# Bias sums at expert pair 9 instead of 12, the last pair's running sums put into PSUM earlier, and the last combine and statistics taken half by half

## The chip, the cores and the metric

The kernel runs on one core of one Trainium2 chip. The metric is the time on the device in microseconds (us). The profile is that of one profiled execution of its own, whose time and span stand beside each other below. TensorE is written PE, its weight loads PEld, VectorE DVE, ScalarE ACT, GpSimd POOL, SyncE SP.

## The reference

One step of a decoder with one layer (`DEPTH` = 1), in float32, for 256 prompt rows and 32 sample rows (8 sequences of 4 tokens), 288 rows of 1024 columns in all:

```python
proj = x @ w_in                         # q, k, v of two head groups
o    = w_out applied to concat(RMSNorm_head(o_A) * gn_moba, RMSNorm_head(o_B) * gn_win)
hx   = LayerNorm(alpha * x + o)         # ln1
logits = hx @ w_router + b_router; the top 4 of 32 experts, softmax over the 4 -> comb (rows x 32)
for each expert e:                      # w_gate_up 1024 x 2048, w_down 1024 x 1024
    gu   = hx @ w_gate_up[e] + b_gate_up[e]
    gate = min(gu[:, 0::2], 7); up = clip(gu[:, 1::2], -7, 7)
    act  = gate * sigmoid(1.702 * gate) * (up + 1)
    acc += comb[:, e] * (act @ w_down[e] + b_down[e])
y    = LayerNorm(alpha * hx + acc)      # ln2
```

The outputs are y for prompt and sample rows and the new key and value rows and window buffers.

## The kernel before

**Stages.** Attention and the first LayerNorm come first. After them the 32 experts are done as 16 pairs (`PAIRS`), numbered 0 to 15; this is most of the time. Each expert takes up to 64 rows (`SLOTS`), so a pair fills 128 slots. If some expert has more than 64 rows, further passes follow (`further_passes`); the profiled execution has none.

**One pair on TensorE.** `gather` picks the pair's rows by a matmul with 0/1 matrices (lines 1051 and 1055). `turn_slots` transposes them, ACT copies them to `xg`. `begin_gate_up` puts the biases of the first projection into banks 0 to 3 (L1267). `gate_up` runs k = 0 to 7, and for each k 8 matmuls 128x64 by 128x512, each of which the trace shows as two instructions (L1171; 64 instructions are four k). DVE and ACT make SwiGLU of it (`swiglu`, `sigmoids`). `turn_act` transposes `up`, ACT copies it to `actT`. `down` runs v = 0 to 3 with two j each (L1224), into banks 4 and 5. ACT copies the result to `ybuf`. `combine` multiplies it by `spread` (the slots' gates, which spread slots over rows): ten matmuls (L1251, L1237), added by DVE to `acc` and `acc_s` (L2080). In a pair that isn't the last, `combine(i)` is issued inside `gate_up(i + 1)` after k = 3.

**The weights.** They come in units of 2 MB, 12 to a pair (u = 0 to 7 the first projection, 8 to 11 the second), into a ring of 9 places (`RING`), all issued by SP in one queue. A unit is issued when the one nine before it has been used (`unit_free`). In pairs 1 to 14 (`load_whole`) two units belong together, and PE waits for both of them ahead of k = 0, 2, 4, 6 and v = 0, 2. In pairs 0 and 15 each unit serves one k or v. Of pair 15, unit 11 comes as two halves, one for each of its j (`load_last_pair`, L523). When `gate_up` of pair 15 is done, the gains and biases of the last LayerNorm are loaded (`load_last`).

**Bias sums.** `finish_with_biases(MIDDLE, ...)` with `MIDDLE` = 12 puts into the `down` of pair 12 the transposition of `comb`, and comb x b_down (plus alpha x ln1_b) for all rows: four 33x128 by 33x512 matmuls and four small ones (`add_biases`, L1122, `add_sample_biases`, L1129). DVE adds them to `acc` (`add_biases`, L2088), and PE waits for that ahead of `gate_up(13)`.

**The last pair (15).** `gate_up` with `combine(14)` after k = 3 and `turn_weights` after k = 5. Then `last_down`: the first half of `up` is transposed (L732), and while ACT copies it PE moves the running sums of tile 0 and of the samples into PSUM by matmuls with the identity (`keep_sums`, L1331 and L1330). After v = 0 and v = 1 the sums of tile 1 follow. Then, when v = 3 is done, ACT copies one half of the result to `ybuf` and DVE the other. `mix_last` adds the combination to the sums in PSUM (L1373), first both halves of tile 0, then the samples, then tile 1. DVE takes the statistics (L2160, L2167), ACT the roots; ACT centres tile 0, DVE multiplies by the gain (L2186), POOL adds the bias, and DVE does samples and tile 1. SP stores.

**Order.** Every engine's program is written out by hand, in order, with semaphores between them. PE never runs past a wait.

Of the kernel before, what the change touches and what calls it, by code (L numbers as in the profile page):

```python
# [109 lines left out]
def build_layer(nc, x_prompt, x_sample, cache_k, cache_v, state_k, state_v, page_table, w_in, gn_moba,  # L110
# [9 lines left out]
    def place(name, shape, at=None, dt=F32):  # L120
# [90 lines left out]
        wout_in2 wout_in3 k_landed0 k_landed1 k_landed2 k_landed3 v_landed0 v_landed1 v_landed2 v_landed3 ln1_in  # L211
# [10 lines left out]
        unit5 unit6 unit7 unit8 unit_used first_in att_in blk_in gn_in bias_in bias_used picked gathered xtok_ready  # L222
# [3 lines left out]
        sums_whole copies_out  # L226
# [100 lines left out]

    def pair_of(p):
        return slice(2 * p, 2 * p + 2) if isinstance(p, int) else bass.ds(p * 2, 2)
# [36 lines left out]
    MIDDLE = 12  # L366
# [35 lines left out]
    def _(sp):  # L402
# [107 lines left out]
        def load_last_pair():  # L510
# [11 lines left out]
            for c in range(2):  # L522
                sp.dma_start(dst[:, :, c, :], src[:, :, 2 + c, :]).then_inc(half_in[8 + c], 16)  # L523
# [22 lines left out]
        sp.dma_start(ln_g[:, :], ln1_g[0:1, :].broadcast_to([128, D])).then_inc(S.ln1_in, 16)  # L546
# [183 lines left out]
    def _(pe):  # L730
# [41 lines left out]
        def mean_squares(n):  # L772
            pe.wait_ge(S.out_taken, n + 1)
            if n == 0:
                pe.wait_ge(S.blk_in, 32)
# [340 lines left out]
        def add_biases(j):  # L1116

            t, half = divmod(j, 2)
            if j == 0:
                pe.wait_ge(S.combT_ready, 2)  # L1120
                pe.wait_ge(S.bdn_in, 32)
# [112 lines left out]
        def mix_samples(out, start):  # L1234

            for q in range(4):
# [86 lines left out]
        finish(MIDDLE + 1, MIDDLE // PERIOD, 1, MIDDLE // PERIOD)  # L1323
        last = PAIRS - 1
        finish(last - 1, last // PERIOD - 1, 2, None)

        def keep_sums(t, half, stop=False):

            if t == 2:
                return nc.tensor.matmul(bank[7][:, 0:256], ident, acc_s[:, :], start=True, stop=stop)  # L1330
            return nc.tensor.matmul(bank[2 * t + half][:, :], ident, acc[:, t, 512 * half:512 * half + 512],  # L1331
                                    start=True, stop=stop)
# [894 lines left out]
```

## Time and profile before

| | us |
|---|---|
| median of 3 runs | 1140.02 |
| lowest, highest | 1139.33, 1140.36 |
| profiled execution | 1139.37 |
| its span | 1137.5 |

| engine | busy us | share |
|---|---|---|
| PE | 1099.5 | 97% |
| DVE | 293.1 | 26% |
| ACT | 203.6 | 18% |
| POOL | 30.0 | 3% |

The span is cut by the page into 40 slices of 28.4 us. From the eighth slice on, its line of DMA rates reads 407 to 433 GB/s, until the last one (160 GB/s). A busy share says how long an engine had an instruction in it, not that the end of the program waits for it. The chain of waits follows the last instruction back to what released it, step by step.

### The profile page before, as it was taken

How to read it: one execution, taken by the hardware profiler on the slowest of the kernel's cores; microseconds unless marked ns; L12 is line 12 of the kernel's file. 1: busy time of each engine (PE TensorE's matmuls, PEld its weight loads, DVE VectorE, ACT ScalarE, POOL GpSimd, SP SyncE). 2: the span in 40 equal slices, each digit the busy share in tenths (PEclk: the TensorE clock that was granted, in tenths of full speed). 3: DMA queues.
4: the chain of work that ended last, by engine and by line, in shares of the span. 5: the costliest groups of instructions: out<-in, count | busy, mean ns of one | idle time of the engine just before them, and what ended most of it. 6: DMA issues, size and time to landing. Idle time of an engine off the chain costs nothing.

```text
span 1137.5 us, 14116 instructions
## 1 busy us (share of the span) xinstructions
PE 1099.5 (97%) x5468; PEld 463.2 (41%) x5469; DVE 293.1 (26%) x734; ACT 203.6 (18%) x481; POOL 30.0 (3%) x65
## 2 busy tenths in 40 slices
PE   8999999999999999999999999999999999999996
PEld 6876764433333333333333333333333333333331
DVE  1553757530303030212121212120203031303033
ACT  2323412411111120202020202020201111111102
POOL 0110111000000000000000000000000000000001
PEclk9999999999999999999999999999999999999998
DMA  9967878999999999999999999999999999999994
GB/s 361 351 219 248 285 280 336 426 433 407 430 421 430 430 431 430 431 430 429 432 431 432 432 430 432 432 432 429 433 430 432 432 430 432 431 430 430 425 426 160
DMA packets 59172, 454.37 MB, mean 399 GB/s; under 512 B 6467, under 2 KB 19411, under 8 KB 31348
## 3 DMA queue, kind: packets, MB, share of 16 engines
q1 hardware_dynamic: 56642, 440.97, 92.7%
q0 software_dynamic: 1728, 10.75, 2.5%
q10 hardware_dynamic: 754, 1.98, 0.4%
q8 instruction: 34, 0.56, 0.2%
q14 instruction: 14, 0.11, 0.0%
HBM read 450.14 MB, written 11.93 MB: 406 GB/s over the span
## 4 chain that ended last, share of the span: by engine, by line
PE 83%; DMA 13%; ACT 2%; DVE 2%; issue 1%; SPq 0%; DVEq 0%
PE bank L1171 30%; PE bank L1224 19%; DMA ring<-in_w_gate_up 13%; PE bank L732 6%; PE bank L759 6%; PE bank L1055 5%; PE bank L1251 3%; PE bank L762 2%; PE bank L920 2%; PE bank L1051 1%; PE bank L1354 1%; PE bank L1267 1%; PE bank L877 1%; ACT ybuf L1417 1%; ACT actT L1417 1%; PE bank L851 1%
## 5 line engine op out<-in xcount | busy, mean ns | idle before, releaser
L1171 PE MATMUL bank<-ring,xg 128*64 128x512 f32 x2032 | 445.6, 594 | 10.8 <-DMA ring<-in_w_gate_up 10.8
L1171 PEld LDWEIGHTS bank<-ring,xg 128*64 128x64 f32 x2032 | 146.4, 137 | 299.3 <-issue 296.9
L1224 PE MATMUL bank<-ring,actT 128*64 128x512 f32 x960 | 216.2, 597 | 4.2 <-ACT actT L1417 4.2
L2080 DVE TENSOR_TENSOR acc<-acc,bank 128x512 f32<-128x512 f32 x60 | 41.3, 688 | 492.0 <-PE bank L1251 491.8
L1571 ACT ACTIVATE sig<-gate 128x256 f32<-128x256 f32 x64 | 26.5, 416 | 530.1 <-DVE gate L2062 530.1
L1224 PEld LDWEIGHTS bank<-ring,actT 128*64 128x64 f32 x960 | 67.3, 137 | 120.0 <-issue 115.3
L2062 DVE TENSOR_SCALAR gate<-bank 128x256 f32<-128x256 f32 x64 | 26.8, 419 | 186.8 <-PE bank L1171 186.8
L759 PE MATMUL bank<-xT,wblk 128*128 128x288 f32 x256 | 65.4, 409 | 0.3 <-DVE xT L1670 0.3
L1562 ACT ACTIVATE xg<-bank,small 128x128 f32<-128x128 f32 x128 | 48.0, 457 | 97.0 <-PE bank L732 96.9
L1055 PE MATMUL bank<-hx,pick 128*128 128x512 f32 x128 | 59.2, 605 | 0.0
L1417 ACT ACTIVATE ybuf<-bank 128x512 f32<-128x512 f32 x63 | 36.0, 596 | 126.7 <-PE bank L1224 87.4
L1251 PE MATMUL bank<-ybuf,spread 128*128 128x512 f32 x120 | 58.4, 619 | 0.0
L759 PEld LDWEIGHTS bank<-xT,wblk 128*128 128x128 f32 x256 | 47.5, 190 | 14.6 <-issue 2.7
L1055 PEld LDWEIGHTS bank<-hx,pick 128*128 128x128 f32 x128 | 23.0, 190 | 34.3 <-issue 34.3
L1251 PEld LDWEIGHTS bank<-ybuf,spread 128*128 128x128 f32 x120 | 19.2, 189 | 39.0 <-DVE acc L2080 19.7
L920 PE MATMUL bank<-wout,outT 128*128 128x512 f32 x64 | 29.8, 603 | 0.0
L762 PE MATMUL bank<-wblk,xT 128*128 128x256 f32 x128 | 29.0, 380 | 0.0
L2066 DVE SCALAR_TENSOR_TENSOR up<-up,gate 128x256 f32<-128x256 f32 x64 | 27.2, 425 | 3.3
L732 PEld LDWEIGHTS bank<-keep,ybuf 128*128 128x128 f32 x128 | 17.8, 207 | 25.3 <-issue 24.3
L723 POOL TENSOR_TENSOR acc<-acc,ln_b_sb 128x512 f32<-128x512 f32 x2 | 3.0, 1500 | 941.0 <-DVE acc L2186 941.0
L2063 DVE TENSOR_SCALAR up<-bank 128x256 f32<-128x256 f32 x64 | 26.5, 414 | 0.0
L2071 DVE TENSOR_TENSOR up<-up,sig 128x256 f32<-128x256 f32 x64 | 25.4, 419 | 0.0
(247 smaller groups left out, 672.3 us busy)
## 6 DMA issues: line engine op xcount, KB each, us to landing
ring<-in_w_gate_up SPq DMA_DIRECT2D x127, 2048.0 KB, 26.5
ring<-in_w_down SPq DMA_DIRECT2D x63, 2048.0 KB, 28.0
wblk<-in_w_in SPq DMA_DIRECT2D x11, 1024.0 KB, 8.7
kring<-in_cache_k_moba SPq DMA_DIRECT2D x16, 256.0 KB, 7.5
vring<-in_cache_v_moba SPq DMA_DIRECT2D x16, 256.0 KB, 7.2
out<-in_state_k_win POOLq DMA_DIRECT2D x8, 512.0 KB, 5.2
out<-in_state_v_win POOLq DMA_DIRECT2D x8, 512.0 KB, 6.1
kring<-in_state_k_win SPq DMA_DIRECT2D x16, 256.0 KB, 5.3
```

The costliest lines, as they stand in the source:

```text
L732: return nc.tensor.transpose(out, in_, ident[0:in_.shape[0], 0:in_.shape[0]])
L759: ins = nc.tensor.matmul(out[:, 0:T], w[:, k, 128 * c:128 * c + 128], xT[:, k, :], start=(k == 0), stop=(k == KC - 1))
L762: ins = nc.tensor.matmul(out[:, 0:256], xT[:, k, 128 * c:128 * c + 128], w[:, k, :], start=(k == 0), stop=(k == KC - 1))
L920: return nc.tensor.matmul(bank[2 * t + half][:, :], outT[:, k, t0:t0 + rows], wout[:, k, 512 * half:512 * half + 512], start=(k == 0), sto ...
L1055: return nc.tensor.matmul(bank[6 + a][:, :], pick[:, t, :], hx[:, t, 512 * a:512 * a + 512], start=False, stop=(t == 1))
L1171: ins = nc.tensor.matmul(bank[n][64 * e:64 * e + 64, :], xg[:, k, 64 * e:64 * e + 64], w[e][:, 512 * n:512 * n + 512], start=False, stop=( ...
L1224: ins = nc.tensor.matmul(bank[4 + half][64 * e:64 * e + 64, :], actT[:, j, 64 * e:64 * e + 64], w[e][:, at:at + 512], start=(j == 0), stop ...
L1251: ins = nc.tensor.matmul(bank[4 + half][:, :], spread[:, t0:t0 + rows], ybuf[:, 512 * half:512 * half + 512], start=True, stop=True)
L1417: return nc.scalar.activation(out, in_, ACT.Copy, **kw)
L1562: ins = nc.scalar.activation(xg[:, k, :], turned, ACT.Identity, bias=s_(c_cols + KC + k), scale=s_(c_cols + k))
L2066: V.scalar_tensor_tensor(up[:, c], up[:, c], 1.0, gate[:, half_of(n)], ALU.add, ALU.mult).then_inc(S.dve_moe, 1)
L2080: V.tensor_tensor(o, o, new, ALU.add).then_inc(S.added, 1)
```

## The change

`MIDDLE` goes from 12 to 9, and the pairs 10 to 13 are then written out behind the loop. In the last pair `combine(14)` comes after k = 1 instead of k = 3, and the sums of tile 0 and the samples are put into PSUM after k = 4 of `gate_up` (`keep_first`) instead of inside `last_down`. The banks of the last pair change for that: the result of `down` goes to banks 0 and 1 (`Y_BANK`), the sums of tile 0 to banks 4 and 5, those of tile 1 to 2 and 3, those of the samples to 7 (`SUM_BANK`); both halves of `up` are transposed through bank 6 (`turn_last`). The part of unit 11 for its second j (1 MB) comes by column halves, as two transfers of 512 KB with rows of 2 KB instead of 4 KB. PE signals when the lower half of `down` is done, ACT copies both halves one after the other (`take_halves`), and DVE copies none. `mix_last` goes half by half: tile 0, tile 1 and two of the samples' quarters of the lower half, then the same of the upper one. DVE takes the lower halves' statistics first. The wait for the last LayerNorm's gains moves down to where they are read. Two semaphores go: `ln1_in` is merged into `bdn_in`, `att_in` into `blk_in`, so what waited for the one transfer now waits for three.

```diff
-    MIDDLE = 12
+    MIDDLE = 9
@@ load_last_pair
-            for c in range(2):
-                sp.dma_start(dst[:, :, c, :], src[:, :, 2 + c, :]).then_inc(half_in[8 + c], 16)
+            sp.dma_start(dst[:, :, 0, :], src[:, :, 2, :]).then_inc(half_in[8], 16)
+            for half in range(2):
+                h = slice(512 * half, 512 * half + 512)
+                sp.dma_start(dst[:, :, 1, h], src[:, :, 3, h]).then_inc((S.lower_in, half_in[9])[half], 16)
@@ sync, scalar
-        sp.dma_start(ln_g[:, :], ln1_g[0:1, :].broadcast_to([128, D])).then_inc(S.ln1_in, 16)
+        sp.dma_start(ln_g[:, :], ln1_g[0:1, :].broadcast_to([128, D])).then_inc(S.bdn_in, 16)
-        act.dma_start(att[:, :], att_table[:, 0:A_END]).then_inc(S.att_in, 16)
+        act.dma_start(att[:, :], att_table[:, 0:A_END]).then_inc(S.blk_in, 16)
...
-                    act.wait_ge(S.att_in, 16)
+                    act.wait_ge(S.blk_in, 48)
...
-                dve.wait_ge(S.att_in, 16)
+                dve.wait_ge(S.blk_in, 48)
...
-            dve.wait_ge(S.ln1_in, 16)
+            dve.wait_ge(S.bdn_in, 48)
@@ tensor: the pairs after the biases
         finish_with_biases(MIDDLE, MIDDLE // PERIOD, 0, MIDDLE // PERIOD)
         finish(MIDDLE + 1, MIDDLE // PERIOD, 1, MIDDLE // PERIOD)
+        finish(MIDDLE + 2, MIDDLE // PERIOD, 2, MIDDLE // PERIOD + 1)
+        finish(MIDDLE + 3, MIDDLE // PERIOD + 1, 0, MIDDLE // PERIOD + 1)
+        finish(MIDDLE + 4, MIDDLE // PERIOD + 1, 1, MIDDLE // PERIOD + 1)
@@ tensor: the last pair
-        def last_down():
-
-            turn_act(last, 2 * last + 2, (0,))
+        def keep_first():
             pe.wait_ge(S.added, 5 * last + 5)
             keep_sums(0, 0)
             keep_sums(0, 1)
-            pe.wait_ge(S.actT_ready, last * 2 + 1)
             keep_sums(2, 0)
+
+        def turn_last(a):
+            pe.wait_ge(S.act_ready, last * 4 + 2 * a + 2)
+            pe.wait_ge(*((S.actT_ready, 2 * last + 1) if a else (S.spread_ready, last + 1)))
+            for j in range(4 * a, 4 * a + 4):
+                f = 512 * a
+                ins = turn(bank[6][:, 128 * (j % 4):128 * (j % 4) + 128], up[:, f + j % 4:f + 512:4])
+            ins.then_inc(S.act_turned, 1)
+
+        def last_down():
+
+            turn_last(0)
...
-                    if v == 3:
-                        pe.wait_ge(half_in[8 + c], 16)
+                    if j == 6:
+                        pe.wait_ge(half_in[8], 16)
                     for half in range(2):
+                        if j == 7:
+                            pe.wait_ge((S.lower_in, half_in[9])[half], 16)
                         for e in range(2):
                             at = 2048 * e + 1024 * c + 512 * half
-                            ins = nc.tensor.matmul(bank[4 + half][64 * e:64 * e + 64, :], actT[:, j, 64 * e:64 * e + 64],
+                            ins = nc.tensor.matmul(bank[Y_BANK[half]][64 * e:64 * e + 64, :], actT[:, j, 64 * e:64 * e + 64],
                                                    w[:, at:at + 512], start=(j == 0), stop=(j == KC - 1))
+                        if j == 7 and half == 0:
+                            ins.then_inc(S.lower_done, 1)
...
-            pe.wait_ge(S.y_ready, last * 2 + 2)
-            for j in (0, 1, 4, 2, 3):
...
+            for half in range(2):
+                pe.wait_ge(S.y_ready, last * 2 + half + 1)
+                for t in range(2):
+                    nc.tensor.matmul(bank[SUM_BANK[t][half]][:, :], spread[:, 128 * t:128 * t + 128],
+                                     ybuf[:, 512 * half:512 * half + 512], start=False, stop=True).then_inc(S.mixed, 1)
+                ins = mix_samples(bank[SUM_BANK[2][0]], False, (2 * half, 2 * half + 1))
+            ins.then_inc(S.mixed, 1)
-        gate_up(last, last // PERIOD, 0, {3: lambda: combine(last - 1), 5: lambda: turn_weights(last, 2 * last + 1)})
+        gate_up(last, last // PERIOD, 0, {1: lambda: combine(last - 1), 4: keep_first, 5: lambda: turn_weights(last, 2 * last + 1)})
@@ scalar
-        def take_lower():
-            act.wait_ge(S.down_done, PAIRS)
-            copy(ybuf[:, 0:512], bank[4][:, :]).then_inc(S.y_ready, 1)
+        def take_halves():
+            for half in range(2):
+                act.wait_ge(*((S.down_done, PAIRS) if half else (S.lower_done, 1)))
+                copy(ybuf[:, 512 * half:512 * half + 512], bank[Y_BANK[half]][:, :]).then_inc(S.y_ready, 1)
@@ vector
-        def take_upper():
-            dve.wait_ge(S.down_done, PAIRS)
-            V.tensor_copy(ybuf[:, 512:1024], bank[5][:, :]).then_inc(S.y_ready, 1)
...
-        dve.wait_ge(S.ln2_in, 160)
         mv = [s_(c_mv + 4 * t, 4) for t in range(3)]
-
-        def y_statistics(t, after):
-            for half in range(2):
-                dve.wait_ge(S.mixed, 5 * last + after + half)
-                step.on(V.bn_stats(s_(c_stat + 12 * t + 6 * half, 6), bank[2 * t + half][:, :]))
-            dve.wait_ge(step.sem, step.n)
+        for t in range(2):
+            dve.wait_ge(S.mixed, 5 * last + t + 1)
+            link(V.bn_stats(s_(c_stat + 12 * t, 6), bank[SUM_BANK[t][0]][:, :]))
+
+        def y_statistics(t):
+            dve.wait_ge(S.mixed, 5 * last + t + 3)
+            link(V.bn_stats(s_(c_stat + 12 * t + 6, 6), bank[SUM_BANK[t][1]][:, :]))
             link(V.bn_aggr(mv[t][:, 0:2], s_(c_stat + 12 * t, 12).rearrange("p (a c) -> p a c", a=2)))
             V.tensor_scalar(mv[t][:, 1:2], mv[t][:, 1:2], LN_EPS, None, ALU.add).then_inc(S.y_varied, 1)
-        y_statistics(0, 1)
-        dve.wait_ge(S.mixed, 5 * last + 3)
+        y_statistics(0)
+        dve.wait_ge(S.mixed, 5 * last + 5)
...
-        y_statistics(1, 4)
+        y_statistics(1)
...
+        dve.wait_ge(S.ln2_in, 160)
         for half in range(2):
             c = slice(512 * half, 512 * half + 512)
             dve.wait_ge(S.y_centred, half + 1)
```

## Rows read from the trace of the kernel before

**Rows 1.** The page's chain that ended last, shares of the span by engine.

```profile
PE 83%; DMA 13%; ACT 2%; DVE 2%; issue 1%; SPq 0%; DVEq 0%
```

**Rows 2.** A stretch: start:end, length, busy us (instructions), clock, DMA, GB/s.

```profile
700.00:800.00 100.00, 95.74 (x433) 34.66 (x435) 14.16 (x32) 13.71 (x32) 0.00 (x0) 1.00 1.01 432
```

**Rows 3.** Timeline of TensorE, first-projection matmuls, pairs 11, 12 and 14.

```profile
862.51 7.09 PE L1171 MATMUL bank<-ring,xg 128*64 128x512 f32 x32 [0.96 <-DMA ring<-in_w_gate_up]
...
920.86 7.09 PE L1171 MATMUL bank<-ring,xg 128*64 128x512 f32 x32 [0.96 <-DMA ring<-in_w_gate_up]
...
1012.26 13.95 PE L1171 MATMUL bank<-ring,xg 128*64 128x512 f32 x64
...
1030.54 14.10 PE L1171 MATMUL bank<-ring,xg 128*64 128x512 f32 x64
```

**Rows 4.** Chain in order of time (start, length, what), pairs 7, 12, 15.

```profile
580.69 1.06 PE bank L1051 x4
...
603.11 1.07 PE bank L1267 x8
...
927.95 1.06 PE bank L1051 x4
...
955.41 1.07 PE bank L1267 x8
...
1068.28 13.88 PE bank L1171 x64
1082.16 3.82 PE bank L1251 x8
...
1104.79 3.58 PE bank L1354 x16
```

**Rows 5.** Issues of the last weights: start times by line.

```profile
L494 SPq DMA_DIRECT2D ring<-in_w_gate_up x8: 367/434/9523, 1026.9 to 1067.2; - x8
...
L523 SPq DMA_DIRECT2D ring<-in_w_down x2: 2944/5823/8702, 1082.7 to 1085.7; - x2
```

**Rows 6.** Their time from issue to landing, issues of 1066:1068 and of 1084:1090.

```profile
ring<-in_w_gate_up SPq DMA_DIRECT2D x1, 2048.0 KB, 29.5
...
ring<-in_w_down SPq DMA_DIRECT2D x2, 1024.0 KB, 31.2
```

**Rows 7.** Timeline of the last pair's end, all engines.

```profile
1101.88 0.75 PE L732 MATMUL bank<-keep,up 128*128 128x128 f32 x4 [0.75 <-DVE up L2071]
...
1102.67 0.60 ACT L1417 ACTIVATE actT<-bank 128x512 f32<-128x512 f32 x1 [1.63 <-PE bank L732]
...
1121.62 0.60 ACT L1417 ACTIVATE ybuf<-bank 128x512 f32<-128x512 f32 x1 [10.42 <-PE bank L1354]
...
1122.37 1.98 PE L1373 MATMUL bank<-ybuf,spread 128*128 128x512 f32 x4 [0.80 <-DVE ybuf L2139]
...
1123.60 1.49 DVE L2160 BATCH_NORM_STATS2 small<-bank 128x6 f32<-128x512 f32 x2 [1.29 <-PE bank L1373]
...
1124.28 0.64 PE L1237 MATMUL bank<-ybuf,spread 128*32 128x256 f32 x8
...
1125.43 0.42 DVE L2167 BATCH_NORM_STATS2 small<-bank 128x6 f32<-128x256 f32 x1
...
1126.51 1.29 DVE L2160 BATCH_NORM_STATS2 small<-bank 128x6 f32<-128x512 f32 x2
...
1128.85 1.29 DVE L2186 TENSOR_TENSOR acc<-acc,ln_g_sb 128x512 f32<-128x512 f32 x2
```

**Rows 8.** The first stretch: length, busy us (instructions) by engine, clock, DMA, GB/s.

```profile
0.00:60.00 60.00, 54.81 (x338) 44.22 (x340) 22.29 (x63) 16.54 (x47) 7.62 (x20) 1.00 0.97 357
```

**Rows 9.** What uses the early tables, and the landing of the last of them.

```profile
L1686 DVE SCALAR_TENSOR_TENSOR headB<-att x16: 546/549/559, 28.9 to 148.6; 128x384 f32<-128x384 f32 x16
...
L1429 ACTq DMA_DIRECT2D heads_of<-in_att_table x1: 454/454/454, 11.7 to 11.7; - x1
...
DMA to landing us min/median/max: 9.2/9.2/9.2
```

More of the change, by code:

```diff
@@ L1232, in down, with mix_samples @@
             ins.then_inc(S.down_done, 1)
-        def mix_samples(out, start):
-            for q in range(4):
+        def mix_samples(out, start, quarters=range(4)):
+            for q in quarters:
                 ins = nc.tensor.matmul(out[NS * q:NS * q + NS, 0:256], spread[:, SEQ:T],
@@ L1329, in keep_sums @@
             if t == 2:
-                return nc.tensor.matmul(bank[7][:, 0:256], ident, acc_s[:, :], start=True, stop=stop)
-            return nc.tensor.matmul(bank[2 * t + half][:, :], ident, acc[:, t, 512 * half:512 * half + 512],
+                return nc.tensor.matmul(bank[SUM_BANK[2][0]][:, 0:256], ident, acc_s[:, :], start=True, stop=stop)
+            return nc.tensor.matmul(bank[SUM_BANK[t][half]][:, :], ident, acc[:, t, 512 * half:512 * half + 512],
                                     start=True, stop=stop)
-        def last_down():
-            turn_act(last, 2 * last + 2, (0,))
+        def keep_first():
             pe.wait_ge(S.added, 5 * last + 5)
@@ L1358, in last_down @@
                 if v == 0:
[L1359 removed]
+                    turn_last(1)
                     keep_sums(1, 0)
@@ L1365, in mix_last @@
         def mix_last():
-            pe.wait_ge(S.y_ready, last * 2 + 2)
-            for j in (0, 1, 4, 2, 3):
-                t, half = divmod(j, 2)
-                if t == 2:
-                    ins = mix_samples(bank[7], False)
-                else:
-                    ins = nc.tensor.matmul(bank[j][:, :], spread[:, 128 * t:128 * t + 128],
-                                           ybuf[:, 512 * half:512 * half + 512], start=False, stop=True)
-                ins.then_inc(S.mixed, 1)
-        gate_up(last, last // PERIOD, 0, {3: lambda: combine(last - 1), 5: lambda: turn_weights(last, 2 * last + 1)})
+            for half in range(2):
[6 more added lines that the diff above has]
+        gate_up(last, last // PERIOD, 0, {1: lambda: combine(last - 1), 4: keep_first, 5: lambda: turn_weights(last, 2 * last + 1)})
         last_down()
@@ L1575, in take_weights, with take_turned @@
             copy(spread[:, :], bank[6][:, 0:T]).then_inc(S.spread_ready, 1)
-        def take_turned(i, halves=(0, 1)):
+        def take_turned(i, halves=(0, 1), banks=(7, 6)):
             for a in halves:
                 act.wait_ge(S.act_turned, i * 2 + (a + 1))
-                copy(actT[:, 4 * a:4 * a + 4, :], bank[7 - a][:, :].rearrange("p (k s) -> p k s", k=4)).then_inc(
+                copy(actT[:, 4 * a:4 * a + 4, :], bank[banks[a]][:, :].rearrange("p (k s) -> p k s", k=4)).then_inc(
                     S.actT_ready, 1)
@@ L1649, in _ @@
         for half in range(2):
-            nc.scalar.activation(acc[:, 0, 512 * half:512 * half + 512], bank[half][:, :], ACT.Identity,
+            nc.scalar.activation(acc[:, 0, 512 * half:512 * half + 512], bank[SUM_BANK[0][half]][:, :], ACT.Identity,
                                  bias=mv[:, 2:3], scale=mv[:, 1:2]).then_inc(S.y_centred, 1)
@@ L2135, in _ @@
         last = PAIRS - 1
-        def take_upper():
-            dve.wait_ge(S.down_done, PAIRS)
-            V.tensor_copy(ybuf[:, 512:1024], bank[5][:, :]).then_inc(S.y_ready, 1)
         def sums_to_sbuf():
-            take_upper()
-            for n, j in enumerate((0, 1, 4, 2, 3)):
+            for n, j in enumerate((0, 2, 1, 3, 4)):
                 t, half = divmod(j, 2)
-                o, new = (acc[:, t, 512 * half:512 * half + 512], bank[j][:, :]) if t < 2 else (acc_s[:, :], bank[7][:, 0:256])
+                o, new = (acc[:, t, 512 * half:512 * half + 512], bank[SUM_BANK[t][half]][:, :]) if t < 2 else (acc_s[:, :], bank[SUM_BANK[2][0]][:, 0:256])
                 dve.wait_ge(S.mixed, 5 * last + n + 1)
@@ L2196, in _ @@
             c = slice(512 * half, 512 * half + 512)
-            gain_and_bias(acc[:, 1, c], bank[2 + half][:, :], mv[1][:, 0:1], mv[1][:, 1:2], ln2_g_sb[:, c], ln2_b_sb[:, c])
+            gain_and_bias(acc[:, 1, c], bank[SUM_BANK[1][half]][:, :], mv[1][:, 0:1], mv[1][:, 1:2], ln2_g_sb[:, c], ln2_b_sb[:, c])
     ctx.close()
```

20 lines of the change are left out of this document (10 added, 10 removed).

## The prediction

> **What bounds the kernel now.** I read the chain of waits first. It gives TensorE 83% and the weights' transfers 13% [rows 1], so one of the two is late at a time, and the question is which, in which pair. The stretches say that the transfers never pause: between 700 and 800 us their share is 1.01 at 432 GB/s while PE is busy 95.74 of 100 us [rows 2]. There the transfers set the pace and PE has some room. The timeline of PE shows where it waits. In pairs 11 and 12 it waits 0.96 us for weights ahead of k = 6, and these starts are 920.86 - 862.51 = 58.35 us apart [rows 3]. That is the stream's own pace for 12 units, 4.86 us each. The same point two pairs later should come at 920.86 + 2 x 58.35 = 1037.56. In pair 14, k = 4 starts at 1030.54, two k take half of the run of four, some 7.0 us, so k = 6 starts at 1037.5 to 1037.7. That run is 14.10 us long where the unhindered one of the same pair is 13.95 [rows 3], so 0.15 us of it is a last wait for weights. By pair 14 PE has then caught up with the stream in spite of the bias sums in pair 12.
>
> From there to the end it is PE's own work. By the issues and their time to landing, unit 7 of pair 15 lands at 1067.2 + 29.5 = 1096.7 and the second half of unit 11 at 1085.7 + 31.2 = 1116.9 [rows 5, 6]. PE's first projection ends at 1101.88 - 0.75 = 1101.13 [rows 7], so its k = 7, 3.5 us long, starts about 1097.6, 0.9 us after its weights. The second projection runs from 1104.79 [rows 4] to 1121.62, where both copies begin [rows 7]. That is 16.83 us. Its last j, half of a 3.58 us v, starts at about 1119.8, 2.9 us after its weights. The end is bound by PE, then by the serial statistics on DVE, and not by transfers.
>
> **Early bias sums.** They cost PE, from the gathering to the next pair's first bias matmul, 955.41 - 927.95 = 27.46 us against 603.11 - 580.69 = 22.42 in pair 7, so 5.0 us [rows 4]. In pair 12 they are given back over pairs 13 and 14, 58.35 - 55.8 = 2.5 us in each, since PE needs 1068.28 - 1012.26 = 56.0 us from the first projection of pair 14 to that of pair 15, wait included [rows 3, 4]. In pair 9 they are given back by pair 12, and pair 14 then waits for its own weights. What comes out is the 0.15 us by which pair 14 was late, and no more: **-0.15 us**. Ends: 0 and -0.2. The writing out of pairs 10 to 13 adds code but no instruction. A pair written out (pair 14) takes 56.0 us here, with its wait, and any looped pair in the bound stretch 58.35, so cover of 2.3 us stands over it: nothing. Without the cover it would cost the difference between such pairs, which no row separates: -0.2 to +0.2 us each.
>
> **combine(14) after k = 1.** The same instructions. The main row is 3.82 us long [rows 4], and k = 2 ends that much later and the samples' 0.6 more. Its ring place is what unit 11 waits for. Before, SP issued unit 11 at 1082.7 [rows 5] since its queue was still pushing unit 10. After, k = 2 ends at 1068.1 + 3 x 3.47 + 4.4 = 1082.9, so the issue is 0.2 us late, and then lies 31 us in the queue [rows 6]: nothing, from 0 to +0.2, which would have to pass the 2.9 us of room first.
>
> **keep_first after k = 4.** The three products moved take 1104.79 - (1101.88 + 0.75) = 2.16 us [rows 4, 7]. In their new place they are on PE's path too, since PE waits for no weights there: +2.16, and the first projection ends at 1103.1. Taken from the old place they give -2.16, but they covered ACT's copy of `actT`. Now PE stands still from the end of the turning until the copy is done: ACT starts 0.03 us after it and takes 0.60 [rows 7], and PE follows by some 0.1: **+0.73 us**. Ends: 0.65 and 1.0. Together this edit brings a loss, as the wait on DVE ahead of the turning (0.75 us, [rows 7]) stays what it was, and the wait on ACT behind it is new. The second turning through bank 6 waits for the first copy, done 3.6 us earlier, and keep_sums(1, 0) covers its own copy as before: 0.
>
> The end of the second projection, E = 1121.62, moves by -0.15 + 2.16 - 2.16 + 0.73 = +0.6, to 1122.2.
>
> **Column halves of unit 11.** The second half must be there when the last j starts, now 1120.4, and lands at about 1117: nothing. A bound on the cost of short rows is the first stretch, 357 GB/s [rows 8] against 432: 2 MB in 5.9 us instead of 4.9, so it lands at most 1.0 us later, at 1118. The loads of gains come 2 us later, as they wait for the first projection. They land before 1124, and are read at 1129. The Trainium skill speaks against such a cut ("DMA: Bandwidth & Descriptors", section "Bandwidth"): its rule is to batch transfers to at least 1 MiB. By that page's anatomy a transfer has some 2.0 us fixed beside bytes over 436 GB/s (given for transfers issued from GpSimd). An estimate from these figures is 2 x 3.2 us for the two pieces against 4.4 for one, 2 us later, so a landing at 1118.9, still before PE asks. In this trace the cost of a cut transfer does not show: SP's two 1 MB halves are spaced by the queue, both 31.2 us from issue to landing [rows 5, 6].
>
> **Last combine, half by half.** Before, PE starts it 0.75 us after E (1122.37): it waited for DVE's copy [rows 7]. Now the lower half is done 0.88 us before E', ACT's copy (0.60) is ready by E', and PE goes on without a stop at E' - 0.1. A matmul of the combine takes (1124.28 - 1122.37) / 2 = 0.95 us, the samples 0.6 for four quarters, 0.3 for two. So tile 0's upper half starts after 2 x 0.95 + 0.3 = 2.2 us, at E' + 2.1, where it started at E + 0.75 + 0.95 = E + 1.7 before. The upper statistics of tile 0 follow a matmul's start by 1.1 us. They ran from 1123.60 + 1.49 - 0.70 = 1124.39, E + 2.77, and start now at E' + 3.2. Going half by half thus starts PE 0.85 us sooner and puts 1.25 us more of it ahead of this point: +0.4.
>
> From that point DVE's chain to the gain was 1128.85 - 1124.39 = 4.46 us [rows 7]. One of tile 1's two statistics has moved ahead of it, 1.29 / 2 = 0.65: 3.81 now. The samples' statistics stood 1125.43 - 1124.39 = 1.04 into it, at E' + 4.24 now, and have to wait for the last mix at E' - 0.1 + 4 x 0.95 + 0.6 + 0.15 = E' + 4.45: +0.2. The gain comes at E' + 3.2 + 3.8 + 0.2 = E' + 7.2, and came at 1128.85 - 1121.62 = E + 7.2. **0**, with ends of -0.5 and +0.5. What is behind the gain is unchanged. What PE gains at the copy is lost again in DVE's order, since the samples now come last on PE and still ahead of tile 1 on DVE, and ACT's centring of tile 0 waits behind them too.
>
> **The merged semaphores.** The slowest of the three tables lands at 11.7 + 9.2 = 20.9 us, and DVE first reads `att` at 28.9 [rows 9]: 0 of 8 us of room. For `bdn_in` the third transfer is the one that DVE waited for already, and the bias sums come hundreds of us later: 0.
>
> **Sum.** -0.15 + 0.73 + 0 = +0.6 us on the profiled execution's 1139.37 us (span 1137.5, 1.9 us around it, unchanged): 1139.97. The median of the runs shown is 0.65 above the profiled one, so 1140.02 + 0.6 = **1140.6 us**. What a measurement of this kernel can tell from no change is about 0.2%, 2.3 us: the forecast is no difference that can be told.
>
> **Rivals.** *Keeping the sums is hidden.* If PE does wait for weights after k = 4 in pair 15, by 2.16 us or more, keep_first costs nothing there, and E moves by -0.15 - 2.16 + 0.73 = -1.6: 1138.4. With the tail at its good end (-0.5) it is 1137.9. For it: the transfers have a share of 1.01 throughout. Against it: k = 7 has 0.9 us of room already without the moved work; each us of work put in front makes PE later. Room would come only if the stream were 3 us later than its pace.
>
> *The bias sums gave more than 0.15.* If the 5.0 us in pair 12 delayed the stream itself (places freed late), all weights behind come earlier now, at most by 2.5 us before PE's own work binds: about 1138. Against it: pair 14's k = 6 comes within 0.1 us of the extrapolated pace.
>
> *Slower: the cut transfers come late.* The place is the last j, the point 1120.4 us. If the last 1 MB, and the gains that now stand close behind it in the same queue, moved at under half the rate, say 184 GB/s for 2.1 MB (11.4 us from 1112), they would land at 1123.4, and the end moves by 3.0 + 0.6 = +3.6: 1143.6. For it: the rows of 2 KB, and the queue shared with loads of 1 KB rows. Against it: short rows brought the first stretch down to 357 and no lower, and 3.5 us of room.
>
> *It doesn't do what it says.* Should the early halves not overlap (ACT busy, or PE held for both), the mix starts 0.6 us later: 1141.2. ACT has nothing else after its second copy of `actT`, so this is unlikely.
>
> **How the numbers follow.** The forecast, with its terms at their ends (-0.2 + 0.65 - 0.5 to +0.2 + 1.0 + 0.5, so 1140.0 to 1141.7) and the case of no early mix, 0.72; keeping hidden 0.10; stream earlier 0.05; late transfers 0.06; what I don't see 0.07, half each way. The faster rivals take the lower end to 1138.3. Above, half a us of spread between runs goes on the forecast's end, so the upper end is 1142.2. Faster by over 0.2% (under 1137.7): a part of the two fast rivals and of the unseen, 0.07. Slower by over 0.2% (over 1142.3): 0.08. Within: 0.85.
>
> **What would show it.** In the profile after: no wait for weights on PE in pair 10 and perhaps 11, and in pair 14 one ahead of k = 2 and k = 6; pair 15's first projection still starting at 1068.1 to 1068.2; its end at about 1103; a wait of 0.7 us on ACT's `actT` ahead of the first v; the second projection's end at 1122.2; the mix starting with no gap; the gain at about 1129.4. A wait for weights in pair 15 after k = 4 would prove the first rival, one ahead of the last j the third; an end of the second projection before 1121 would make the prediction wrong.

## The result, and the profile after

The changed kernel takes 1145.36 us in the median (1143.95 to 1147.44, 6 runs) against 1140.34 for the one before (1139.33 to 1142.12, 6 runs) beside it. The ratio is 1.0039, 95% interval 1.0029 to 1.0049. The forecast was no difference that can be told; the kernel became slower, by 5.0 us in the medians. Timed once more, on another chip, the ratio was 1.0022 (1.0013 to 1.0031).

The profiled execution took 1145.18 us, its span is 1142.9: 5.4 more than before. First the chain of waits of the changed kernel by engine. Weights have a larger share than in [rows 1].

```profile
PE 81%; DMA 15%; ACT 2%; DVE 1%; issue 1%; SPq 0%; DVEq 0%
```

The timeline of TensorE in the changed kernel; these are some of the starts of k = 2 and k = 6 that waited for weights. (Lines have moved by 4 and more: L1175 is the first projection, L1228 the second, L1372 the last pair's.)

```profile
689.33 7.09 PE L1175 MATMUL bank<-ring,xg 128*64 128x512 f32 x32 [0.95 <-DMA ring<-in_w_gate_up]
...
747.67 7.09 PE L1175 MATMUL bank<-ring,xg 128*64 128x512 f32 x32 [0.94 <-DMA ring<-in_w_gate_up]
...
864.92 7.09 PE L1175 MATMUL bank<-ring,xg 128*64 128x512 f32 x32 [0.49 <-DMA ring<-in_w_gate_up]
...
903.73 7.09 PE L1175 MATMUL bank<-ring,xg 128*64 128x512 f32 x32 [1.07 <-DMA ring<-in_w_gate_up]
...
924.03 7.09 PE L1175 MATMUL bank<-ring,xg 128*64 128x512 f32 x32 [1.81 <-DMA ring<-in_w_gate_up]
...
982.58 7.09 PE L1175 MATMUL bank<-ring,xg 128*64 128x512 f32 x32 [1.25 <-DMA ring<-in_w_gate_up]
...
1021.65 7.09 PE L1175 MATMUL bank<-ring,xg 128*64 128x512 f32 x32 [1.32 <-DMA ring<-in_w_gate_up]
...
1041.15 7.09 PE L1175 MATMUL bank<-ring,xg 128*64 128x512 f32 x32 [1.00 <-DMA ring<-in_w_gate_up]
```

Read the starts of k = 6 as a clock of the stream. In [rows 3] they were 58.35 us apart, and 233.4 from pair 8 (687.47) to pair 12 (920.86). Here 689.33 to 924.03 is 234.7, and pair 14 comes at 1041.15, 351.8 after pair 8, where before it came after some 350.1. The wait of 1.81 in pair 12 is the largest; from pair 8 on, none of before is over 1.30. The bias sums in pair 9 cost what they did in pair 12 [rows 4]: 782.21 - 754.75 = 27.46 us.

The chain of the last pair in the changed kernel, in order of time:

```profile
754.75 1.06 PE bank L1055 x4
...
782.21 1.07 PE bank L1271 x8
...
1071.88 7.02 PE bank L1175 x32
...
1083.29 10.45 PE bank L1175 x48
1093.73 1.91 PE bank L1338 x4
1096.08 3.58 PE bank L1175 x16
1100.21 4.46 PE bank L1175 x20
1109.51 3.65 PE bank L1372 x16
...
1134.32 1.29 DVE acc L2201 x2
```

From the first projection's start to the second projection's it takes 37.63 us, where [rows 4] give 36.51. From that same start to DVE's gain it takes 62.44, where before it took 1128.85 - 1068.28 = 60.57 [rows 4, 7]. The timeline around the end, all engines, against [rows 7]:

```profile
1107.98 0.75 PE L736 MATMUL bank<-keep,up 128*128 128x128 f32 x4 [0.75 <-DVE up L2090]
...
1108.77 0.60 ACT L1435 ACTIVATE actT<-bank 128x512 f32<-128x512 f32 x1 [1.63 <-PE bank L736]
...
1109.51 1.08 PE L1372 MATMUL bank<-ring,actT 128*64 128x512 f32 x4 [0.78 <-ACT actT L1435]
...
1125.55 0.60 ACT L1435 ACTIVATE ybuf<-bank 128x512 f32<-128x512 f32 x1 [9.56 <-PE bank L1372]
...
1126.29 1.98 PE L1390 MATMUL bank<-ybuf,spread 128*128 128x512 f32 x4
1126.41 0.60 ACT L1435 ACTIVATE ybuf<-bank 128x512 f32<-128x512 f32 x1 [0.26 <-PE bank L1372]
...
1128.20 0.63 PE L1241 MATMUL bank<-ybuf,spread 128*32 128x256 f32 x4
...
1128.76 1.98 PE L1390 MATMUL bank<-ybuf,spread 128*128 128x512 f32 x4
...
1129.99 0.70 DVE L2175 BATCH_NORM_STATS2 small<-bank 128x6 f32<-128x512 f32 x1 [0.91 <-PE bank L1390]
...
1131.35 0.43 DVE L2181 BATCH_NORM_STATS2 small<-bank 128x6 f32<-128x256 f32 x1 [0.23 <-PE bank L1241]
```

So the 5.4 us of the two profiles are: 2.2 up to the first projection of pair 0 (220.72 against 218.55), 1.7 in the stream from pair 8 to pair 14 (1.3 of it by pair 12), 1.9 in the last pair, and -0.4 in what is left.

### The profile page after: what moved, and what is told of

It reads as the page before. It is cut to its first block, busy times and chain, and to the rows that moved or that the text cites. A ratio compares the mean times of both kernels' runs of the same rounds, so it can differ in the third digit from the quotient of the medians.

```text
span 1142.9 us, 14105 instructions
## 1 busy us (share of the span) xinstructions
PE 1103.0 (97%) x5468; PEld 465.6 (41%) x5469; DVE 292.8 (26%) x733; ACT 204.1 (18%) x482; POOL 30.0 (3%) x65
## 4 chain that ended last, share of the span: by engine, by line
PE 81%; DMA 15%; ACT 2%; DVE 1%; issue 1%; SPq 0%; DVEq 0%
PE bank L1175 28%; PE bank L1228 19%; DMA ring<-in_w_gate_up 15%; PE bank L736 6%; PE bank L763 6%; PE bank L1059 5%; PE bank L1255 3%; PE bank L766 2%; PE bank L924 2%; PE bank L1055 1%; PE bank L1372 1%; PE bank L881 1%; PE bank L1271 1%; ACT actT L1435 1%; ACT ybuf L1435 1%; PE bank L855 1%
## 5 line engine op out<-in xcount | busy, mean ns | idle before, releaser
L1175 PE MATMUL bank<-ring,xg 128*64 128x512 f32 x2032 | 445.9, 594 | 11.9 <-DMA ring<-in_w_gate_up 11.9
L1175 PEld LDWEIGHTS bank<-ring,xg 128*64 128x64 f32 x2032 | 146.8, 137 | 299.8 <-issue 299.4
L1228 PE MATMUL bank<-ring,actT 128*64 128x512 f32 x960 | 216.1, 597 | 4.2 <-ACT actT L1435 4.2
L1228 PEld LDWEIGHTS bank<-ring,actT 128*64 128x64 f32 x960 | 67.5, 137 | 119.8 <-issue 115.6
L1255 PE MATMUL bank<-ybuf,spread 128*128 128x512 f32 x120 | 58.4, 618 | 0.0
L736 PE MATMUL bank<-keep,up 128*128 128x128 f32 x128 | 19.7, 296 | 6.0 <-ACT ybuf L1435 5.2
```

What stands on the lines that cost most here:

```text
L736: return nc.tensor.transpose(out, in_, ident[0:in_.shape[0], 0:in_.shape[0]])
L1175: ins = nc.tensor.matmul(bank[n][64 * e:64 * e + 64, :], xg[:, k, 64 * e:64 * e + 64], w[e][:, 512 * n:512 * n + 512], start=False, stop=( ...
L1255: ins = nc.tensor.matmul(bank[4 + half][:, :], spread[:, t0:t0 + rows], ybuf[:, 512 * half:512 * half + 512], start=True, stop=True)
```

## Experiments

Each kernel ran beside the kernel before on the same chip. Total times scatter by 1 to 2 us from run to run, as much as most of these effects, so the verdicts rest on distances between marks of a profile. "Start" is when the first projection of pair 0 begins. "Stream" is k = 6 of pair 8 to k = 6 of pair 12. "Then" is from there to the first projection of the last pair. "Last pair" is the start of its first projection to DVE's gain. Stream and last pair repeat within 0.2 us where the code concerned is the same. Start and "then" don't: they differ by up to 2.2 us and 1.6 us between kernels with the same code there.

| kernel | ratio to before (95%) | start | stream | then | last pair |
|---|---|---|---|---|---|
| before | | 218.6 | 233.4 | 147.4 | 60.57 |
| changed | 1.0039 (1.0029-1.0049) | 220.7 | 234.7 | 147.9 | 62.44 |
| changed, again | 1.0022 (1.0013-1.0031) | 220.6 | 234.9 | 147.3 | 62.44 |
| b_bias9 | 1.0010 (1.0001-1.0019) | 220.8 | 234.9 | 147.3 | 60.56 |
| b_written_out | 1.0016 (1.0007-1.0025) | 220.7 | 234.8 | 148.9 | 60.55 |
| a_bias12 | 1.0012 (1.0004-1.0021) | 220.8 | 233.4 | 147.4 | 62.44 |
| b_merged | 1.0003 (0.9994-1.0012) | 220.5 | 233.4 | 148.2 | 60.55 |
| a12_keep_back | 1.0005 (0.9995-1.0014) | 219.1 | 233.4 | 148.9 | 61.25 |
| a12_mix_whole | 1.0010 (1.0000-1.0020) | 220.7 | 233.4 | 148.8 | 61.75 |
| b_early_lower | 0.9991 (0.9982-1.0001) | 219.1 | 233.4 | 147.4 | 60.12 |
| best | 0.9999 (0.9990-1.0008) | 218.8 | 233.4 | 147.3 | 60.89 |
| b_bias2 | 1.0006 (0.9996-1.0015) | 220.4 | 231.1 | 148.9 | 60.55 |
| b_bias2_single14 | 0.9990 (0.9980-0.9999) | 219.1 | 231.8 | 145.6 | 62.84 |
| best2 | 0.9989 (0.9980-0.9998) | 219.1 | 231.1 | 144.9 | 61.03 |

In the last three kernels PE is 5 us behind from pair 2 on and catches up with the stream only in pair 9, so their stretch from pair 8 is shorter and isn't compared.

**Bias sums early, and code written out.** b_bias9 is the kernel before with the first two edits of the change alone:

```diff
-    MIDDLE = 12
+    MIDDLE = 9
+        finish(MIDDLE + 2, ...)
+        finish(MIDDLE + 3, ...)
+        finish(MIDDLE + 4, ...)
```

> The kernel before with MIDDLE = 9 alone, pairs 10 to 13 written out behind the loop. Theory A (code fetches): the three more pairs written out bring about six 16 KB instruction fetches into the stretch where weights set the pace, which the looped code had none of, and each holds up one of the 16 transfer engines: from pair 8 to pair 14 the k = 6 starts are 351.5 to 352 us apart instead of 350.1, so +1.3 to +1.7 us. Rival B (the early bias sums themselves delay the stream, code has no part): the same total, but the delay stands in the two intervals behind pair 9. Rival C (the stream is only different from run to run): +0.0, 350.1 us. All three leave the end of the last pair as in before: gain 60.6 us after the first projection of pair 15 starts.

b_written_out leaves the bias sums where they were and only cuts the loop:

```diff
-        with pe.Fori(1, MIDDLE // PERIOD) as m:
+        with pe.Fori(1, 3) as m:
             finish_three(m)
+        finish_three(3)
```

> The kernel before with the bias sums left in pair 12, but pairs 9, 10 and 11 written out behind a shorter loop on PE. Theory A (code fetches): instruction fetches appear from 700 us on, and the k = 6 start of pair 12 comes 1.0 to 1.5 us later relative to pair 8 (234.4 to 234.9 us instead of 233.4); total +0.5 to +1.5 us. Rival B (early bias sums delay the stream): no bias sums are moved, so 233.4 us and +0.0. Rival C (run to run): 233.4 us and +0.0.

The TensorE timeline of b_written_out, then one of its stretches (columns as in [rows 2]):

```profile
689.44 7.09 PE L1171 MATMUL bank<-ring,xg 128*64 128x512 f32 x32 [0.95 <-DMA ring<-in_w_gate_up]
...
747.78 7.09 PE L1171 MATMUL bank<-ring,xg 128*64 128x512 f32 x32 [0.96 <-DMA ring<-in_w_gate_up]
...
807.64 8.78 PE L1171 MATMUL bank<-ring,xg 128*64 128x512 f32 x32 [2.36 <-DMA ring<-in_w_gate_up]
...
865.85 7.09 PE L1171 MATMUL bank<-ring,xg 128*64 128x512 f32 x32 [0.50 <-DMA ring<-in_w_gate_up]
...
924.21 7.09 PE L1171 MATMUL bank<-ring,xg 128*64 128x512 f32 x32 [0.96 <-DMA ring<-in_w_gate_up]
...
808.00:809.00 1.00, 1.00 (x6) 0.35 (x4) 0.00 (x0) 0.00 (x0) 0.00 (x0) 0.82 0.99 426
809.00:810.00 1.00, 1.00 (x4) 0.30 (x2) 0.00 (x0) 0.00 (x0) 0.00 (x0) 0.50 1.11 475
812.00:813.00 1.00, 1.00 (x8) 0.45 (x6) 0.00 (x0) 0.00 (x0) 0.00 (x0) 0.97 1.00 426
```

From 747.78 to 807.64 is 59.86 us, 1.5 more than the pace, after which the pace is 58.2 and 58.4 again. No bias sum is near: they stand in pair 12. b_bias9 has its step at 925.41, after a wait of 2.47. So rival B falls, and rival C with it: four profiles of kernels written out lose 1.3 to 1.5 us by pair 12, and seven of looped kernels lose nothing there. The totals of b_bias9 and b_written_out rise by 1 to 2 us, the looped b_merged by 0.3, within its interval.

What the code does to the stream is in the DMA queues. First those of the kernel before, then those of the changed one, each for 700 to 920 us; then those of b_written_out for 801 to 802 us, 6 us before the late unit:

```profile
q1 hardware_dynamic: 6515, 94.88, 100.7%
...
q1 hardware_dynamic: 6502, 94.64, 100.5%
q8 instruction: 6, 0.10, 0.2%
```

```profile
q8 instruction: 1, 0.02, 6.0%
```

The looped kernel fetches no instructions from about 570 us, when the loop's first round is over, until it leaves the loop at 940. The changed kernel fetches six times from 700 to 920 us, 16 KB each. One of them is 6.0% of 16 engines in 1 us, about 0.96 us of one engine.

The traces tie the steps to the fetches. Units land 4.8 to 4.9 us apart. In b_written_out a fetch starts at 801.4, and the unit due some 5 us after the one at 801.2 lands at 807.5, 6.3 after it. Between 640 and 1060 us the fourteen traces have 13 landings that come over 5.6 us after the one before; every one follows a fetch by 2.5 to 6.1 us, and there is none in a stretch without fetches. Most of the 93 fetches of that time are followed by none. Meanwhile the transfers don't pause: from 800 to 820 us b_written_out moved 431 GB/s, before 430.

How a fetch makes a unit late is argued and not shown. If a unit counts as landed only when all 16 engines have brought their part, one engine that is 0.96 us late delays it, and at a share of 1.01 it finds no idle time to catch up in. That would fit with the unbroken rate, and the steps would come on those fetches only that fall on an engine that is already late. The profile doesn't tell the engines apart, and a step of up to 1.5 us is more than one fetch. That written out code makes the step by pair 12 is shown.

The same is seen in the looped kernels once they have left the loop, from 940 us on, where all fourteen kernels fetch. In a12_keep_back a fetch starts just after 1000 us (its queue from 1000 to 1001 us, then PE's timeline), and k = 6 of pair 14 comes 118.16 us after that of pair 12, where before it came after 116.7:

```profile
q8 instruction: 1, 0.02, 5.5%
```

```profile
1039.73 7.09 PE L1175 MATMUL bank<-ring,xg 128*64 128x512 f32 x32 [0.95 <-DMA ring<-in_w_gate_up]
```

Three of the seven looped kernels lose 0.7 to 1.5 us in this way (column "then"). So from pair 8 to pair 14 it is 350.0 to 351.5 us in looped kernels, and 351.5 to 353.0 in those written out: 1.4 us more in the mean, but the two ranges touch, and what one execution pays varies.

**The changed kernel with the bias sums in pair 12.**

> The changed kernel with MIDDLE back at 12, all else as changed. Theory A and rival B both: 1.4 to 1.7 us less than the changed kernel, so +3.0 to +3.6 us over before with a start of the usual length. Rival C: as the changed kernel, +5. In all of them the last pair keeps its own loss: gain 62.4 us after the first projection of pair 15 starts, against 60.6 in before.

The stream is back at 233.4, and 62.44 us of the last pair stay. Its ratio, 1.0012, is +1.4 us (0.5 to 2.4), and the 1.9 us of the last pair fit into that. The expected +3.0 to +3.6 was too high. It is what the changed kernel's first +5.0 leaves without the stream's 1.4 to 1.7, with the late start still in it. From pair 12 to the last pair's first projection it takes 147.4 us (924.40 to 1071.83), as before. So a gain from early bias sums doesn't show.

**The semaphores.**

> The kernel before with only the two semaphores merged (att_in into blk_in, ln1_in into bdn_in). Theory: nothing waits longer, +0.0 us, and the 2.1 us by which the profile of the changed kernel is later after the first 20 us is a difference of single executions (the matmuls between 9.5 and 14 us went at half their pace there). Rival D: the merging or another edit of the start costs the 2.1 us every time, so +2.1 us here, with the first 32 projection matmuls in 10.0 us instead of 8.0.

Its start is 220.5, so by this one run rival D was open. Over all 14 profiles the start is 218.6 to 219.1 in six and 220.4 to 220.8 in eight. Kernels with the merged semaphores are on both sides (a12_keep_back and b_early_lower 219.1, a_bias12 220.8), and so are those without (before 218.6, b_bias9 220.8), so rival D falls. The first 32 projection instructions take 8.00 us in some executions and 9.8 to 10.2 in others, as the chains of before and after show:

```profile
9.30 8.00 PE bank L759 x32
...
9.51 9.97 PE bank L763 x32
```

It is TensorE's clock. In seven of the eight late ones the instructions behind the first start 0.48 us apart and go over to 0.24 us at 13 to 14 us; in the other profiles they are 0.24 apart from the second on. The traces' records of the granted clock begin at the same places, with full speed: at 13.0 to 13.8 us in these seven, at 8.1 to 9.1 in the others. The eighth, b_bias2, had its first 32 in 8.00 us. It lost its 2 us later, when the granted clock was at the lower level, 1.2 GHz, from 213.8 to 217.2 us. Its stretch around that, then the same stretch of the kernel before (columns as in [rows 2]):

```profile
211.00:218.00 7.00, 7.00 (x25) 3.66 (x26) 5.28 (x24) 2.03 (x3) 0.00 (x0) 0.76 1.01 425
...
211.00:218.00 7.00, 6.89 (x31) 3.82 (x31) 5.71 (x25) 3.32 (x6) 0.00 (x0) 1.00 1.01 425
```

**The last pair, edit by edit.** Both start from a_bias12. a12_keep_back:

```diff
-        gate_up(last, ..., {1: lambda: combine(last - 1), 4: keep_first, 5: ...})
+        gate_up(last, ..., {3: lambda: combine(last - 1), 5: ...})
             turn_last(0)
+            keep_first()
             for v in range(4):
```

> The changed kernel with MIDDLE = 12, and in the last pair combine(14) again after k = 3 and the three keep_sums of tile 0 and the samples again between the first turning and the second projection. Theory A (the moved sums uncover ACT's copy): the second projection ends 53.4 us after the first projection starts, as in before (53.3), not 54.5, and the wait on actT is gone: -1.1 us against a_bias12, gain at 61.3. Rival B (the banks or the turning through bank 6 cost it): stays at 54.5.

The gain came at 61.25, a change of -1.19; the second projection started 1106.97 - 1070.46 = 36.51 us after the first, as in before to the hundredth. Theory A holds. The run puts back combine(14) as well, but its place costs PE nothing: it holds PE for 4.38 us both after k = 3 and after k = 1 (1082.10 to 1086.48 before, 1078.83 to 1083.21 in the changed kernel). a12_mix_whole puts back the two copies at once, the order tile 0, samples, tile 1, and the order of the statistics:

```diff
-            for half in range(2):
-                pe.wait_ge(S.y_ready, last * 2 + half + 1)
...
+            pe.wait_ge(S.y_ready, last * 2 + 2)
+            for j in (0, 1, 4, 2, 3):
```

> The changed kernel with MIDDLE = 12, and the last combine and statistics in the old manner: both copies at once on ACT and DVE when the second projection is done, tile 0, samples, tile 1. Theory A (the half-by-half order makes DVE's chain wait for the last samples' product): from the end of the second projection to the gain 7.2 us as in before, not 7.9, so -0.7 us against a_bias12, though PE starts the combine 0.75 us later. Rival B (the tail is bound by ACT's centring or the banks): stays at 7.9.

```profile
1072.23 7.02 PE bank L1175 x32
...
1126.76 0.70 DVE ybuf L2156
...
1133.98 1.29 DVE acc L2203 x2
```

From the copy to the gain is 7.22 us, as before (7.23), and -0.69 in all. With 1.19 and 0.69 the 1.87 of the last pair are accounted for.

**The part that helps, alone.** b_early_lower is the kernel before, in which ACT copies the lower half when its last j is done (with two semaphores freed by the merging), DVE the upper one, and the order of the combine stays:

```diff
+                        if j == 7 and half == 0:
+                            ins.then_inc(S.lower_done, 1)
...
-            pe.wait_ge(S.y_ready, last * 2 + 2)
+            pe.wait_ge(S.lower_taken, 1)
             for j in (0, 1, 4, 2, 3):
+                if j == 1:
+                    pe.wait_ge(S.y_ready, last * 2 + 2)
```

> The kernel before (with the two merged semaphores, which free the two that it needs) and one thing from the change: ACT copies the lower half as soon as its last j is done, DVE the upper one, and the combine keeps its old order and starts with tile 0's lower half at once. Theory: the combine moves up by 0.75 to 0.85 us and the whole chain behind it too, gain at 59.7 to 59.8 us after the first projection starts instead of 60.56. Rival: DVE's chain binds, so 60.5.

From the end of the second projection (the upper copy, 1122.43) to the gain (1129.07) it takes 6.64 us instead of 7.23, so -0.59, less than the 0.75 to 0.85 expected. The last pair is shorter by 0.45 only: the other 0.14 went in its first projection, whose last two k took 7.23 us instead of 7.09. The time is 0.9991 of before (0.9982 to 1.0001), which is not clear of no change.

**Looking for a version that wins.** best takes MIDDLE = 12, the early lower half, the sums and combine(14) early as in the change, and single units in pair 14:

```diff
+        for u in range(UNITS):
+            unit_free(4, 2, u, WHOLE if u < RING else LATE)
+            load_unit(PAIRS - 2, 2, u)
```

> MIDDLE = 12, early lower half with the old order of the combine, the sums early (after k = 4) and combine(14) after k = 1 as in the change, and pair 14 loaded and used in single units as pair 15 is, so that its k = 6 doesn't wait for unit 7. Theory: PE is held only at k = 7 of pair 14, 3.5 us less of its own work stands behind the last wait, the sums moved into the first projection fill room that is now there: first projection of pair 15 starts 3.5 us sooner against the stream, waits for units 6 and 7, the second projection ends 1.5 to 2.9 us sooner than in before, the gain 2.3 to 3.7 us sooner. Rival: single units come slower or PE waits at each k of pair 14, and no more than the 0.8 us of the early lower half is left.

It missed: 0.9999 (0.9990 to 1.0008). Behind k = 6 of pair 12 PE waited for no weights, since with 5 us of bias sums in pair 12 its own work was just as late as the stream. Room in pair 14 can be used only if PE is early there. That gives the early bias sums a use, if they cost no written out code: pair 2 stands in written out code ahead of the loop already.

```diff
-    MIDDLE = 12
+    MIDDLE = 2
...
-        finish(2, 0, 2, 1)
+        finish_with_biases(2, 0, 2, 1)
+        with pe.Fori(1, 4) as m:
+            finish_three(m)
+        finish(12, 4, 0, 4)
...
```

> The kernel before with the bias sums in pair 2, ahead of the loop over pairs 3 to 11, so that they are early and no pair more is written out. Theory A (only code written out slows the stream): the k = 6 starts stay 58.35 us apart through pair 12, pair 14 then waits for its weights, and the first projection of pair 15 starts 147.4 us after pair 12's k = 6 as in before (147.4), or up to 1.5 us later if code fetches behind pair 12 hit the slowest transfer engine: +0 to +1.5 us. Rival B (early bias sums delay the stream by their lateness): the stream is late by 1 us or more already at pair 12. In neither is anything gained, since the wait of pair 14 follows.

> b_bias2 with pair 14 loaded and used in single units. Theory: early bias sums are worth something only when PE is kept by the stream in pair 14 and can use its room there: PE waits at k = 7 alone, so the first projection of pair 15 starts up to 3.5 us sooner against the stream, then waits for units 6 and 7 of pair 15; the second projection ends 0.9 to 1.5 us sooner than in before against the stream. Rival: as b_bias2, +0.

> best with the bias sums in pair 2. Theory: all of it together, PE kept by the stream at k = 7 of pair 14, the moved sums in the room of pair 15's first projection, and the early lower half: second projection ends some 2 us, the gain some 3 us sooner than in before against pair 12's k = 6 (205 us instead of 208.0), so -2 to -3 us, less up to 1.5 us of fetches. Rival: the stream itself ends late and binds, or PE doesn't get ahead: no more than -0.6 us (the early lower half).

The timeline of TensorE in b_bias2 and the chain of best2:

```profile
922.94 7.09 PE L1171 MATMUL bank<-ring,xg 128*64 128x512 f32 x32 [0.95 <-DMA ring<-in_w_gate_up]
...
981.30 7.09 PE L1171 MATMUL bank<-ring,xg 128*64 128x512 f32 x32 [0.97 <-DMA ring<-in_w_gate_up]
...
1041.12 7.09 PE L1171 MATMUL bank<-ring,xg 128*64 128x512 f32 x32 [2.43 <-DMA ring<-in_w_gate_up]
```

```profile
1066.50 7.02 PE bank L1180 x32
...
1104.12 3.65 PE bank L1374 x16
...
1120.97 1.92 PE bank L1397 x4
...
1127.53 1.29 DVE acc L2211 x2
```

b_bias2 (1.0006, 0.9996 to 1.0015) keeps the pace from pair 9 through pair 13 with the sums in pair 2, so early sums alone don't slow the stream. Between 981.30 and 1041.12 a step of 1.5 us comes, in the stretch where this kernel has left the loop. b_bias2_single14 comes to 0.9990 (0.9980 to 0.9999), but by the marks it missed what was expected: the first projection of pair 15 starts 1.8 us sooner against pair 12's k = 6, then waits 1.22 and 0.41 us for weights, and the second projection ends 0.5 us later than before instead of 0.9 to 1.5 sooner. best2 is at 1140.40 against 1141.67, 0.9989 (0.9980 to 0.9998): from pair 12's k = 6 (921.62) to the gain it takes 205.9 us, before 208.0. It is the fastest here by these marks. In the medians it is faster than the kernel before by 1.3 us (0.2 to 2.3), and the expected -2 to -3 us wasn't reached; the marks account for 2.1.

**The changed kernel again.**

> The changed kernel once more, beside the kernel before on the same chip. By the marks of the profiles, the changed kernel is later by 1.4 to 1.7 us in the stream (code written out) and by 1.9 us in the last pair, +3.3 to +3.6 us; the 2.2 us of its first 20 us are one of two starts that both kernels have. So the medians should be 3 to 4 us apart, a ratio of 1.0026 to 1.0035. Rival D (the start belongs to the change): 5 us or more, 1.0044 and up, and again a first gate_up at 220.7 us. The last pair again takes 62.4 us from the first projection to the gain, and the k = 6 starts of pairs 8 and 14 are 351.5 us or more apart.

The stream (351.5 us from pair 8 to 14) and the last pair (62.44) repeat. The ratio, 1.0022, came out below the expected 1.0026 to 1.0035, whose lower part its interval holds. The first measurement's, 1.0039, is above it, and the two intervals meet only at 1.0029 to 1.0031: +3.3 to 3.5 us, which agrees with the marks (1.3 to 1.5 and 1.9). Both its profiles have the late start, so that the changed kernel has it more often is not excluded.

## Why the prediction was wrong

The forecast was +0.6 us. The two measurements are +5.0 (3.3 to 5.6) and +2.5 (1.5 to 3.5); what the experiments tie to the change is +3.3, 1.4 in the stream by pair 12 and 1.9 in the last pair.

*Early bias sums, -0.15.* Right as a mechanism: 27.46 us again, given back by pair 11, and PE waits in pair 14, 1.32 us at k = 2 and 1.00 at k = 6. The -0.15 itself is less than the steps vary by.

*Written out code, "cover of 2.3 us stands over it: nothing".* This is the step that failed. I looked for its cost on PE, where the wait for weights covers anything up to 2.3 us. It fell on the stream, which is itself the bound and has no cover: 1.3 to 1.5 us by pair 12. The query on the DMA queues has a row for instruction fetches, and the looped stretch has none of them. I didn't ask what a loop saves. The pair that I took for the price, pair 14 at 56.0 us, is written out, but had hardly to wait for the stream, so it couldn't show this cost.

*keep_first, +0.73.* The mechanism was right, the size wrong: the second projection starts 1.12 us later and ends 1.19 later. The uncovered copy was 0.78 (the wait on `actT` in the timeline). In their new place the sums took 1096.08 - 1093.73 = 2.35 us, and the first projection as a whole grew by 2.5, where 2.16 was put: the run of matmuls is interrupted once more, and that cost 0.3 us here.

*Last combine, 0.* Mis-sized as well: +0.69. PE did start at once (1126.29). But two quarters of the samples cost 1128.76 - 1128.20 = 0.56 us, as four had cost before, 1124.85 - 1124.28 = 0.57 [rows 7]: the 0.3 taken for them was a division by instructions. The row behind those four quarters in the timeline of before:

```profile
1124.85 1.99 PE L1373 MATMUL bank<-ybuf,spread 128*128 128x512 f32 x4
```

In that trace the four quarters run side by side: each is two instructions of some 0.4 us, and the four first ones start within 0.02 us, as the four second ones do. Half of them saves nothing. So the upper statistics started 3.58 us and not 3.2 after E' (1126.41), and the samples' statistics 4.94 and not 4.45.

*Column halves, merged semaphores: 0.* Nothing contradicts it, and by a_bias12, a12_keep_back and a12_mix_whole no part of the last pair is left for the halves. The last piece landed at 1119.8, and the last j began at about 1124.6. The halves were not tried alone.

*The range.* The half us that I allowed for spread between runs was too small: the kernel before went from 1139.1 to 1144.2 in later runs, and the profile of it that I read was one of the early starts. The late start, 2.2 us in the profile shown, belongs here too: kernels without the change have it as well. The rivals all missed the stream's own cost.

*The signs.* The waits in pair 14, the one on `actT` and the mix without a gap came as written. Pair 15's first projection came at 1071.88 and not at 1068.1 to 1068.2, which is the late start and the stream together, and took 35.4 us instead of 35.0.

## What to carry to other kernels

Where a stream of transfers is the bound, ask of each edit what it adds to that stream, instruction fetches of unrolled code included: a cover on the engine that waits doesn't count there. Work moved onto an engine that has room is worth nothing until the wait behind it can be used; here that took smaller units in the pair with the last wait. A half of a small step may cost as much as the whole, so look in the trace whether the parts ran side by side before counting a half at half price. And compare like stretches of code: one profile's start and its straight code differed here by 1 to 2 us from run to run.

## What the runs showed of the hardware

A 16 KB instruction fetch took 0.88 to 0.96 us of one transfer engine (5.5% and 6.0% of 16 engines in 1 us), and pairs run from a loop's second round needed none for 370 us. With the weights' transfers at a share of 1.01, 13 of 93 fetches were followed within 2.5 to 6.1 us by a unit that landed over 5.6 us after the one before, instead of 4.8 to 4.9.

Four matmuls 128x32 by 128x256 into different rows of one bank ran side by side: four cost 0.57 us and two 0.56.

TensorE's full clock began at 8.1 to 9.1 us in seven profiles and at 13.0 to 13.8 in the other seven, and 32 instructions of the projection took 8.00 or 9.8 to 10.2 us accordingly. After PE had stood still for 2.36 us in b_written_out, the granted clock fell from 1.00 to 0.50, the lower level of 1.2 GHz, between 808 and 812 us, and the 32 instructions of k = 6 and 7 took 8.78 us instead of 7.09. The same followed waits of 2.27 us (changed, again) and 2.47 us (b_bias9). It didn't follow the wait of 2.43 us in b_bias2, nor that of 1.81 us in the changed kernel: there they took 7.09.
